# Input norm of a hybrid decoder layer: the reciprocal roots moved from VectorE's weighting into TensorE's transposing products

## The chip, the cores and the metric

The kernel runs on one core of one Trainium2 chip. The metric is device time in microseconds (us) of one execution. TensorE (PE in the rows) has a separate row for its weight loads (PEld); VectorE is DVE, ScalarE is ACT, GpSimd is POOL, and SyncE (SP) issues nearly all DMAs.

## The reference, cut to what matters

The reference is one decoder layer: 16 meta tokens and 512 real tokens of width 1024 are normalized, projected by one wide matrix, sent through sliding-window attention and a gated linear attention in parallel, merged, added to the stream, and then sent through a mixture of experts. The change concerns only the first step:

```python
def rms_norm(x, w):
    xf = x.astype(jnp.float32)
    y = xf * lax.rsqrt(jnp.mean(xf * xf, axis=-1, keepdims=True) + NORM_EPS)
    return (y * w.astype(jnp.float32)).astype(x.dtype)
...
    xn = rms_norm(h, norm1_w)
    proj = xn @ w_in
```

Each token (row) has one reciprocal root, and each of the 1024 columns has one weight. For the projection the kernel needs the normalized x transposed, with the 1024 columns on partitions.

## The kernel before, in words

The 512 real tokens are four blocks (b = 0 to 3) of 128 tokens, one token to a partition, held in `h`. The normalized stream is kept transposed and in two parts: `xhi`, x rounded to the fp32r format that TensorE multiplies in one pass, and `xlo`, the rest. Every projection is three products, hi by hi, hi by lo and lo by hi (lines 617 to 619).

All engines walk one list of steps, `SCHEDULE`, each engine in that order, and they meet only at semaphores. The list begins `xin`, `prep 0`, `xT`, `prep 1`, `xm 0`, then the first units of the projection. So an engine that waits in a step holds up all of its later steps.

- `xin` before the change. TensorE spreads the norm weights over 128 partitions (line 690), and ScalarE copies them to `norm1_b` (line 1271). For each block, ScalarE squares `h` and sums the squares (line 1275), VectorE turns the sum into mean plus epsilon (line 1575), GpSimd raises that to the power of -1/2 (line 1985, recorded at the helper's line 1952), and VectorE forms `xr = h * rstd * norm1_b` in one instruction (line 1578). VectorE does the means of blocks 0 and 1 ahead of `xr` of block 0, and after that the mean of block b + 1 ahead of `xr` of block b.
- `prep 0`: ScalarE and VectorE split the small gate weights into hi and lo (`gdp`, lines 1251 and 1567). `prep 1` splits the first wide chunk of weights, in two halves each.
- `xT`: for each block, TensorE transposes `xr` in eight 128x128 pieces, four to a PSUM bank (line 699); ScalarE copies each bank to `xhi` (line 1281), and VectorE writes the difference to `xlo` and so empties the bank (line 1585). Eight banks hold the eight halves.
- `xm`: the same for the meta tokens. ScalarE squares them after `prep 1`, GpSimd makes their root and then builds the rotary tables, VectorE scales them (line 1594), and TensorE transposes them after the first units (line 706).
- The first units (function `first_units`, lines 645 to 660) wait until all of `xhi` is there, and for a bank that line 1585 empties last.

DMAs: SP issues four loads of `h`, two weight chunks, the meta tokens and 16 small constants. Later weight chunks are issued when VectorE has done with the chunk whose buffer they take.

Of the kernel before, what the change touches and what calls it, by code (L numbers as in the profile page):

```python
# [21 lines left out]
ALU = mybir.AluOpType  # L22
ACT = mybir.ActivationFunctionType
# [3 lines left out]
D = 1024  # L27
T = 512
P = 128
NB = T // P  # L30
# [10 lines left out]
EPS = 1e-6  # L41
# [133 lines left out]
EARLY_DMAS = 2  # L175
# [89 lines left out]
def layer_kernel(nc, x, meta_tokens, norm1_w, w_in, q_norm_w, k_norm_w, attn_sinks, gla_gate_up, gla_gate_bias,  # L265
                 gla_norm_w, w_attn_branch, w_gla_branch, w_out, norm2_w, router_rows, norm2_rows,
                 expert_w_gate, expert_w_up, expert_w_down, table, triangle, rows_hbm, out):
    with ExitStack() as ctx:
# [3 lines left out]
        def sem(name):  # L272
            return ctx.enter_context(nc.semaphore(name))


        h = sb("h", [P, NB, D])
# [13 lines left out]
        stat = sb("stat", [P, 16])  # L290
        rstd = sb("rstd", [P, 16])
# [5 lines left out]
        ident = C("ident")  # L297
# [5 lines left out]
        def at(name, offset, shape, dt=F32):  # L303
            size = int(np.prod(shape[1:])) * 4
            assert offset + size <= arena_size, (name, offset, size, arena_size)
            return nc.alloc_sbuf_tensor_at(name, shape, dt, offset=arena_start + offset)

        K1 = 1024
# [5 lines left out]
        G = 82 * K1  # L314
# [30 lines left out]
        xr = at("xr", Y, [P, NB, D])  # L345
# [36 lines left out]
        norm1_b = at("norm1_b", G + 24 * K1, [P, D])  # L382
        norm1_1 = at("norm1_1", G + 28 * K1, [1, D])
        gdT = at("gdT", G + 64 * K1 + 256 + 4 * K1 + 512, [RANK + 1, XC])
        g_l = g_q1
        xj = at("xj", G + 32 * K1, [NM, D])
        reset = at("reset", Y + 16 * K1, [P, T])


# [47 lines left out]
        s_x = [sem(f"x{b}_loaded") for b in range(NB)]  # L437
        s_meta = sem("meta_loaded")
        s_early = sem("table_loaded")
# [14 lines left out]
        s_sumsq = sem("x_squares_summed")  # L454
        s_mean = sem("x_means")
        s_rstd = sem("x_rstd")
        s_xr = sem("x_scaled")
        s_xhi = sem("xT_hi")
        s_xlo = sem("meta_xT_lo")
        s_l = sem("log_terms")  # L460
# [152 lines left out]
        def _(pe):  # L613
# [15 lines left out]
            link = chain(pe, s_pe)  # L629
# [55 lines left out]
            for step in SCHEDULE:  # L685
                kind = step[0]
                if kind == "xin":
                    for half in range(2):
                        ps = banks.take(pe, "unit", ("norm1", half))
                        nc.tensor.matmul(ps[:, :], ones[0:1, :].bitcast(F32), norm1_1[:, half * 512:(half + 1) * 512],  # L690
                                         start=True, stop=True).then_inc(banks.done(("norm1", half)), 1)
                elif kind == "xT":
                    for b in range(NB):
                        pe.wait_ge(s_xr, b + 1)
                        for half in range(2):
                            ps = banks.take(pe, "x", ("xT", b, half))
                            for k in range(4):
                                src = xr[:, b, :].rearrange("p (c k) -> p k c", k=KT)[:, 4 * half + k, :]
                                last = nc.tensor.transpose(ps[:, k * P:(k + 1) * P], src, ident)
                            last.then_inc(banks.done(("xT", b, half)), 1)  # L700
                elif kind == "xm" and step[1] == 1:
                    pe.wait_ge(s_xr, NB + 1)
                    ps = banks.take(pe, "T", "xmT")
                    for k in range(KT):
                        src = xm[:, :].rearrange("p (c k) -> p k c", k=KT)[:, k, :]
                        last = nc.tensor.transpose(ps[:, k * NM:(k + 1) * NM], src, ident[0:NM, 0:NM])
                    last.then_inc(banks.done("xmT"), 1)
                elif kind == "unit":
# [17 lines left out]
                    if name == "gd":  # L726
                        ps = banks.take(pe, "unit", step)
                        last = mm3(ps[0:RANK, 0:NM], cols(gd_hi, 0, RANK), cols(gd_lo, 0, RANK),
                                   cols(xm_hi, 0, NM), cols(xm_lo, 0, NM), KT)
                    elif meta:  # L730
                        ps = banks.take(pe, "unit", step)
                        last = mm_packed(ps[0:PACK, 0:n], xpm, cols(wh, 0, n), cols(wl, 0, n))
                    elif name in ("qg", "ga", "gg", "kg"):
                        ps = banks.take(pe, "unit", step)
                        a, b = u * P, (u + 1) * P
                        last = mm3(ps[:, :], cols(wh, a, b), cols(wl, a, b), cols(xhi, xa, xb), cols(xlo, xa, xb), KT)
                    elif name in ("vg", "kva", "qa", "rg"):
                        ps = banks.take(pe, "unit", step)
                        a, b = NM + u * P, NM + (u + 1) * P
                        last = mm3(ps[:, 0:n], cols(xhi, a, b), cols(xlo, a, b), cols(wh, 0, n), cols(wl, 0, n), KT)  # L740
                    elif name in ("wa", "wg"):
                        if u == 0 and c0 == 0:
                            for b in range(NB):
                                pe.wait_ge(*banks.emptied(("ogT" if name == "wg" else "oT", b)))
                        ih, il = (oghi, oglo) if name == "wg" else (ohi, olo)
                        ps = banks.take(pe, "unit", step)
                        last = mm3(ps[:, :], cols(wh, u * P, (u + 1) * P), cols(wl, u * P, (u + 1) * P),
                                   cols(ih, 0, T), cols(il, 0, T), 4)
                    else:
                        ps = banks.take(pe, "unit", step)  # L750
                        last = mm3(ps[:, 0:n], tokens(mhi, u), tokens(mlo, u),
                                   cols(wh, 0, n), cols(wl, 0, n), KT)
                    last.then_inc(banks.done(step), 1)
                elif kind == "gates":
# [3 lines left out]
                    ps = banks.take(pe, "unit", ("z", j))  # L758
                    nc.tensor.matmul(ps[:, :], gate_up[:, j * P:(j + 1) * P], gdT[:, NM:XC],
                                     start=True, stop=True).then_inc(banks.done(("z", j)), 1)  # L760
# [3 lines left out]
                    ps = banks.take(pe, "T", "zm")  # L764
                    for j in range(2):
                        last = nc.tensor.matmul(ps[:, j * NM:(j + 1) * NM], gate_up[:, j * P:(j + 1) * P],
                                                gdT[:, 0:NM], start=True, stop=True)
                    last.then_inc(banks.done("zm"), 1)
                elif kind == "kdm":
                    pe.wait_ge(s_exp, 5)  # L770
                    ps = banks.take(pe, "T", "kdm")
                    for j in range(2):
                        last = nc.tensor.transpose(ps[0:NM, j * P:(j + 1) * P], lm[:, j, :], ident)
# [434 lines left out]
        def _(act):  # L1208
# [29 lines left out]
            for step in SCHEDULE:  # L1238
# [27 lines left out]
                elif kind == "xin":  # L1266
# [5 lines left out]
                                             ACT.Copy).then_inc(banks.read(("norm1", half)), 1)  # L1272
                    for b in range(NB):
                        act.wait_ge(s_x[b], 16)
                        nc.scalar.activation(xr[:, b, :], h[:, b, :], ACT.Square,
                                             accum_out=stat[:, b:b + 1]).then_inc(s_sumsq, 1)
                elif kind == "xT":
                    for b in range(NB):
# [217 lines left out]
        def _(dve):  # L1496
# [59 lines left out]
            for step in SCHEDULE:  # L1556
# [11 lines left out]
                elif kind == "xin":  # L1568
                    for half in range(2):
                        dve.wait_ge(*banks.emptied(("norm1", half)))  # L1570
                    for b in range(NB):
                        for ahead in (0, 1) if b == 0 else (b + 1,):
                            if ahead < NB:
                                dve.wait_ge(s_sumsq, ahead + 1)
                                nc.vector.tensor_scalar(stat[:, ahead:ahead + 1], stat[:, ahead:ahead + 1], 1.0 / D, EPS,
                                                        ALU.mult, ALU.add).then_inc(s_mean, 1)
                        dve.wait_ge(s_rstd, b + 1)
                        nc.vector.scalar_tensor_tensor(xr[:, b, :], h[:, b, :], rstd[:, b:b + 1], norm1_b[:, :],
                                                       ALU.mult, ALU.mult).then_inc(s_xr, 1)
                elif kind == "xT":  # L1580
                    for b in range(NB):
                        for half in range(2):
# [364 lines left out]
        def _(pool):  # L1947
# [3 lines left out]
            def tt(o, a, b, op=ALU.mult):  # L1951
                return nc.gpsimd.tensor_tensor(o, a, b, op)  # L1952
# [26 lines left out]
            for step in SCHEDULE:  # L1979
                kind = step[0]  # L1980
                if kind == "xin":
                    pool.wait_ge(s_set, 2)
                    for b in range(NB):
                        pool.wait_ge(s_mean, b + 1)
                        tt(rstd[:, b:b + 1], stat[:, b:b + 1], minus_half[:, b:b + 1], ALU.pow).then_inc(s_rstd, 1)
                elif kind == "xm" and step[1] == 0:
                    pool.wait_ge(s_mean, NB + 1)
                    tt(rstd[0:NM, NB:NB + 1], stat[0:NM, NB:NB + 1], minus_half[0:NM, 0:1], ALU.pow).then_inc(s_rstd, 1)
                    pool.wait_ge(s_early, EARLY_DMAS * 16)
                    pool.wait_ge(s_const, (CONST_DMAS - EARLY_DMAS) * 16)  # L1990
# [128 lines left out]
```

## Time and profile before

| | us |
|---|---|
| median of 3 runs (665.67 to 666.65) | 665.88 |
| the profiled execution's own time | 665.99 |
| its span, first to last instruction | 664.2 |
| TensorE busy | 644.5 |
| VectorE busy | 390.1 |
| ScalarE busy | 214.6 |
| GpSimd busy | 107.8 |

The span is 1.8 us shorter than the execution's own time; what lies around it is outside the profile. The page gives for each engine its busy time, its share of the span and its number of instructions. A row of the timeline reads: start, duration, engine, line, operation, output<-inputs, shape, count, and in brackets the idle time before it and what ended it. Rows of neighbouring instructions of the same kind are merged, with their count behind an x.

### The profile page before, as it was taken

What the parts mean: (1) busy time and instruction counts of PE and PEld (TensorE: products, weight loads), DVE (VectorE), ACT (ScalarE), POOL (GpSimd) and SP (SyncE); (2) the same over time, 40 slices, a digit from 0 to 9 for tenths busy, and PEclk for the clock granted to TensorE, in tenths of its full rate; (3) what the DMA queues carried; (4) which work ended last, traced back from release to release, by engine and by line L of the source; (5) the groups of instructions that cost most, each with busy time, mean ns of one, the idle gap of its engine ahead of it and who ended that gap; (6) DMA issues with size and microseconds to landing.
All of it is one profiled execution on the core that took longest, in us unless ns stands there. A gap on an engine that the chain in (4) does not pass through costs nothing.

```text
span 664.2 us, 10048 instructions
## 1 busy us (share of the span) xinstructions
PE 644.5 (97%) x3887; PEld 459.1 (69%) x3887; DVE 390.1 (59%) x721; ACT 214.6 (32%) x436; POOL 107.8 (16%) x168
## 2 busy tenths in 40 slices
PE   5799999999999999999989999999999999999998
PEld 3579999998787878778789995454444445453535
DVE  4648335688997979776765567444353535261605
ACT  6346222224444343432435475202020111110112
POOL 3300006899400000000000010201010101010010
PEclk9899999999999999999999999999999999999999
DMA  7432222302232211111554076999999999999943
GB/s 246 151 126 65 64 65 77 114 1 64 65 104 81 70 65 63 64 64 64 172 195 174 33 282 241 419 399 423 400 422 395 420 398 420 406 415 406 415 183 126
DMA packets 49793, 138.77 MB, mean 209 GB/s; under 512 B 6202, under 2 KB 28235, under 8 KB 41556
## 3 DMA queue, kind: packets, MB, share of 16 engines
q1 hardware_dynamic: 47298, 134.44, 53.1%
q0 software_dynamic: 2304, 3.64, 1.5%
q8 instruction: 31, 0.51, 0.3%
q14 instruction: 14, 0.11, 0.0%
q10 hardware_dynamic: 146, 0.07, 0.0%
HBM read 138.69 MB, written 4.19 MB: 215 GB/s over the span
## 4 chain that ended last, share of the span: by engine, by line
PE 87%; DVE 6%; ACT 3%; issue 2%; DMA 1%; POOL 0%; ACTq 0%; DVEq 0%
PE bank L1008 16%; PE bank L617 13%; PE bank L618 12%; PE bank L619 12%; PE bank L1022 8%; PE bank L1132 8%; PE bank L859 1%; DVE y_lo L1928 1%; PE bank L1033 1%; PE bank L961 1%; PE bank L892 1%; PE bank L927 1%; ACT whi L1251 1%; DVE sig_a L1637 1%; DVE sig_a L1633 1%
## 5 line engine op out<-in xcount | busy, mean ns | idle before, releaser
L1008 PE MATMUL bank<-w_pair,xgT 128*64 128x512 f32 x512 | 113.8, 596 | 0.0
L1008 PEld LDWEIGHTS bank<-w_pair,xgT 128*64 128x64 f32 x512 | 35.2, 137 | 66.4 <-issue 65.4
L1567 DVE TENSOR_TENSOR wlo<-wraw,whi 128x2048 fp32r<-128x2048 f32 (+1 forms) x25 | 56.4, 2258 | 19.9 <-ACT whi L1251 19.9
L617 PE MATMUL bank<-whi,xhi 128*128 128x256 f32 x224 | 64.4, 287 | 0.0
L619 PE MATMUL bank<-whi,xlo 128*128 128x256 f32 x224 | 62.9, 281 | 0.0
L618 PE MATMUL bank<-wlo,xhi 128*128 128x256 f32 x224 | 62.9, 281 | 0.0
L617 PE MATMUL bank<-xhi,whi 128*128 128x512 f32 x152 | 62.3, 410 | 0.0
L618 PE MATMUL bank<-xlo,whi 128*128 128x512 f32 x152 | 60.1, 395 | 0.0
L619 PE MATMUL bank<-xhi,wlo 128*128 128x512 f32 x152 | 59.7, 393 | 0.0
L1022 PE MATMUL bank<-w_pair,hT 128*64 128x512 f32 x256 | 58.1, 595 | 0.0
L1905 DVE SCALAR_TENSOR_TENSOR hg<-bank,pair_w,hs 128x256 f32<-128x256 f32 x16 | 7.7, 484 | 80.9 <-ACT hs L1472 80.9
L1251 ACT ACTIVATE whi<-wraw 128x2048 fp32r<-128x2048 f32 (+1 forms) x25 | 46.7, 1872 | 24.9 <-PE bank L626 11.1
L1472 ACT ACTIVATE hs<-bank 128x256 f32<-128x256 f32 x16 | 6.1, 383 | 135.6 <-PE bank L1008 135.6
L1941 DVE TENSOR_TENSOR h<-h,bank 128x512 f32<-128x512 f32 x64 | 41.4, 684 | 7.6 <-PE bank L1132 6.1
L1132 PE MATMUL bank<-y_hi,onehotT 128*128 128x512 f32 x112 | 44.2, 395 | 1.5 <-DVE y_lo L1928 1.5
L1132 PE MATMUL bank<-y_lo,onehotT 128*128 128x512 f32 x112 | 43.7, 390 | 0.0
L1928 DVE TENSOR_TENSOR y_lo<-bank,y_hi 128x512 fp32r<-128x512 f32 x32 | 20.6, 686 | 39.1 <-ACT y_hi L1485 39.1
L617 PEld LDWEIGHTS bank<-whi,xhi 128*128 128x128 f32 x224 | 42.1, 188 | 1.8 <-issue 1.4
L1952 POOL TENSOR_TENSOR pause<-pause 128x1 f32<-128x1 f32 x34 | 5.9, 195 | 223.2 <-PE bank L1002 184.2
L619 PEld LDWEIGHTS bank<-whi,xlo 128*128 128x128 f32 x224 | 42.2, 188 | 0.0
L618 PEld LDWEIGHTS bank<-wlo,xhi 128*128 128x128 f32 x224 | 42.1, 188 | 0.0
L1022 PEld LDWEIGHTS bank<-w_pair,hT 128*64 128x64 f32 x256 | 17.7, 137 | 33.3 <-issue 33.3
(333 smaller groups left out, 1304.7 us busy)
## 6 DMA issues: line engine op xcount, KB each, us to landing
w_pair<-in_expert_w_gate SPq DMA_DIRECT2D x32, 1024.0 KB
w_pair<-in_expert_w_up SPq DMA_DIRECT2D x32, 1024.0 KB
w_pair<-in_expert_w_down SPq DMA_DIRECT2D x32, 1024.0 KB, 17.5
wraw<-in_w_in SPq DMA_DIRECT2D x17, 1024.0 KB, 5.5
wraw<-in_w_out SPq DMA_DIRECT2D x4, 1024.0 KB, 5.1
h<-in_x SPq DMA_DIRECT2D x4, 512.0 KB, 5.1
wraw<-in_w_gla_branch SPq DMA_DIRECT2D x2, 1024.0 KB, 5.4
wraw<-in_w_attn_branch SPq DMA_DIRECT2D x2, 1024.0 KB, 5.1
```

Source lines behind the costliest of these rows:

```text
L617: nc.tensor.matmul(ps, lhi(k), rhi(k), start=(k == 0), stop=False)
L618: nc.tensor.matmul(ps, lhi(k), rlo(k), start=False, stop=False)
L619: last = nc.tensor.matmul(ps, llo(k), rhi(k), start=False, stop=(k == kt - 1))
L859: nc.tensor.matmul(ps[:, 0:width], q, k, start=True, stop=True).then_inc(banks.done(("S", b, i, j)), 1)
L1008: last = nc.tensor.matmul(tiles[GU_BANK[s]][j * SLOT:(j + 1) * SLOT, :].rearrange("p (f n) -> p f n", f=2), xgT[:, k, s * P + j * SLOT:s * ...
L1022: last = nc.tensor.matmul(tiles[DOWN_BANKS[s][half]][j * SLOT:(j + 1) * SLOT, :], hT[s][:, f, j * SLOT:(j + 1) * SLOT], we[s][j][2][:, f, ...
L1132: last = nc.tensor.matmul(tiles[SCATTER_BANKS[u % 4]][:, :], onehotT[i % 3][s][:, b, :], part[s][:, cols_], start=(s == 0 and part is y_hi ...
L1251: nc.scalar.activation(wh, raw, ACT.Copy).then_inc(s_hi, 1)
L1567: nc.vector.tensor_tensor(wl, raw, wh.bitcast(F32), ALU.subtract).then_inc(s_lo, 1)
L1905: nc.vector.scalar_tensor_tensor(hg[s][:, :], tiles[GU_BANK[s]][:, FF:2 * FF], pair_w[:, 2 * i + s:2 * i + s + 1], hs[s][:, :], ALU.mult, ...
L1928: last = nc.vector.tensor_tensor(y_lo[s][:, cols_], tiles[DOWN_BANKS[s][half]][:, :], y_hi[s][:, cols_].bitcast(F32), ALU.subtract)
L1941: nc.vector.tensor_tensor(h[:, b, cols_], h[:, b, cols_], tiles[bank][:, :], ALU.add).then_inc(s_add[u % 4], 1)
```

## The change: what it does and the diff

VectorE no longer waits for the roots: as soon as a block of x and the spread weights are there, it forms `xr = h * norm1_b`. ScalarE squares with a scale of 1/32, so that the sum is already the mean. GpSimd adds epsilon (a new tiny instruction), takes the power, and writes for each block a 128x128 matrix `diag` with the block's reciprocal roots on its diagonal (identity times root, spread over 128 columns). TensorE multiplies each piece of `xr` with `diag` where it had used its transpose operation with the identity. The result is the transposed piece with every token scaled. The squares go to a buffer of their own, since `xr` is now written at the same time.

```diff
+        x_sq = at("x_sq", G, [P, NB, D])
+        diag = at("diag", G + 16 * K1, [P, NB, P])
+        eps = at("eps", G + 18 * K1, [P, 1])
...
                     for b in range(NB):
                         pe.wait_ge(s_xr, b + 1)
+                        pe.wait_ge(s_diag, b + 1)
...
-                                last = nc.tensor.transpose(ps[:, k * P:(k + 1) * P], src, ident)
+                                last = nc.tensor.matmul(ps[:, k * P:(k + 1) * P], src, diag[:, b, :], start=True, stop=True)
...
-                        nc.scalar.activation(xr[:, b, :], h[:, b, :], ACT.Square,
+                        nc.scalar.activation(x_sq[:, b, :], h[:, b, :], ACT.Square, scale=D ** -0.5,
                                              accum_out=stat[:, b:b + 1]).then_inc(s_sumsq, 1)
...
                     for b in range(NB):
-                        for ahead in (0, 1) if b == 0 else (b + 1,):
-                            if ahead < NB:
-                                dve.wait_ge(s_sumsq, ahead + 1)
-                                nc.vector.tensor_scalar(stat[:, ahead:ahead + 1], stat[:, ahead:ahead + 1], 1.0 / D, EPS,
-                                                        ALU.mult, ALU.add).then_inc(s_mean, 1)
-                        dve.wait_ge(s_rstd, b + 1)
-                        nc.vector.scalar_tensor_tensor(xr[:, b, :], h[:, b, :], rstd[:, b:b + 1], norm1_b[:, :],
-                                                       ALU.mult, ALU.mult).then_inc(s_xr, 1)
+                        dve.wait_ge(s_x[b], 16)
+                        nc.vector.tensor_tensor(xr[:, b, :], h[:, b, :], norm1_b[:, :], ALU.mult).then_inc(s_xr, 1)
...
                 if kind == "xin":
                     pool.wait_ge(s_set, 2)
+                    pool.wait_ge(s_early, EARLY_DMAS * 16)
+                    link(nc.gpsimd.memset(eps[:, :], EPS))
                     for b in range(NB):
-                        pool.wait_ge(s_mean, b + 1)
+                        pool.wait_ge(s_sumsq, b + 1)
+                        link(tt(stat[:, b:b + 1], stat[:, b:b + 1], eps[:, :], ALU.add))
                         tt(rstd[:, b:b + 1], stat[:, b:b + 1], minus_half[:, b:b + 1], ALU.pow).then_inc(s_rstd, 1)
+                        pool.wait_ge(s_rstd, b + 1)
+                        tt(diag[:, b, :], ident, rstd[:, b:b + 1].to_broadcast([P, P])).then_inc(s_diag, 1)
                 elif kind == "xm" and step[1] == 0:
-                    pool.wait_ge(s_mean, NB + 1)
+                    pool.wait_ge(s_mean, 1)
```

`link` makes the engine wait for the instruction that it has just issued; the two waits of GpSimd inside a block (for the sum, for the root) therefore put its three instructions strictly one behind the other.

## Rows read from the trace of the kernel before

**Rows 1.** The page: busy time by engine, then shares of the chain that ended last.
```profile
PE 644.5 (97%) x3887; PEld 459.1 (69%) x3887; DVE 390.1 (59%) x721; ACT 214.6 (32%) x436; POOL 107.8 (16%) x168
PE 87%; DVE 6%; ACT 3%; issue 2%; DMA 1%; POOL 0%; ACTq 0%; DVEq 0%
```
**Rows 2.** The chain of waits from 9 us on: start, duration, what.
```profile
9.47 1.54 POOL rstd L1952
...
15.51 4.80 DVE xlo L1585 x8
...
20.44 3.32 PE bank L645 x8
...
31.45 0.98 PE bank L706 x8
```
**Rows 3.** Timeline of ScalarE and VectorE, 6 to 21 us.
```profile
6.54 0.60 ACT L1271 ACTIVATE norm_b<-bank 128x512 f32<-128x512 f32 x1 [1.11 <-PE bank L690]
7.98 0.19 ACT L1275 ACTIVATION_READ_ACCUMULATOR xr<-h 128x1 f32 x1
10.50 1.06 ACT L1275 ACTIVATE xr<-h 128x1024 f32<-128x1024 f32 x1 [0.18 <-DMA h<-in_x]
16.10 1.08 ACT L1281 ACTIVATE xhi<-bank 128x512 fp32r<-128x512 f32 x2 [0.26 <-PE bank L699]
...
8.32 0.15 DVE L1575 TENSOR_SCALAR stat<-stat 128x1 f32<-128x1 f32 x1 [6.97 <-ACT xr L1275]
9.31 1.28 DVE L1578 SCALAR_TENSOR_TENSOR xr<-h,rstd,norm_b 128x1024 f32<-128x1024 f32 x1
20.21 1.22 DVE L1563 TENSOR_TENSOR wlo<-wraw,whi 128x1024 fp32r<-128x1024 f32 x1
```
**Rows 4.** Timeline of GpSimd: a root alone, a root and a square product later.
```profile
8.63 0.57 POOL L1952 TENSOR_TENSOR rstd<-stat,minus_half 128x1 f32<-128x1 f32 x1 [6.57 <-DVE stat L1575]
27.09 0.40 POOL L1952 TENSOR_TENSOR tri_r<-k_tok 128x128 fp32r<-128x128 f32 x1
L1952 POOL TENSOR_TENSOR pause<-pause 128x1 f32<-128x1 f32 x34 | 5.9, 195 | 223.2 <-PE bank L1002 184.2 <-DVE row_no L1553 28.1 <-issue 9.8
```
**Rows 5.** Timelines where GpSimd and VectorE meet: 117 to 131 us, then 23 us.
```profile
117.77 1.66 POOL L1952 TENSOR_TENSOR rstd<-stat,minus_half 128x8 f32<-128x8 f32 x1 [7.29 <-DVE stat L1509]
125.75 3.52 POOL L1952 TENSOR_TENSOR rstd<-stat,minus_half 128x8 f32<-128x8 f32 x1 [0.96 <-DVE stat L1509]
...
125.49 2.29 DVE L1567 TENSOR_TENSOR wlo<-wraw,whi 128x2048 fp32r<-128x2048 f32 x1
127.69 0.29 DVE L1625 TENSOR_SCALAR rgs<-rgs 128x256 f32<-128x256 f32 x1
...
23.26 3.30 DVE L1594 TENSOR_SCALAR xm<-xm,rstd 16x1024 f32<-16x1024 f32 x1 [0.65 <-POOL rstd L1952]
23.20 2.81 POOL L1952 TENSOR_TENSOR tab<-cst,qk_w 128x256 f32<-128x256 f32 x4
```
**Rows 6.** Timeline of TensorE's weight loads and products, narrow stretches.
```profile
2.73 3.78 PE L690 MATMUL bank<-norm,ones 1*128 1x512 f32 x4 [2.73 <-DMA norm<-in_norm_w]
...
10.64 1.97 PE L699 MATMUL bank<-cst,xr 128*128 128x128 f32 x8 [4.14 <-DVE xr L1578]
10.92 1.30 PEld L699 LDWEIGHTS bank<-cst,xr 128*128 128x128 f32 x6
13.93 0.99 PEld L699 LDWEIGHTS bank<-cst,xr 128*128 128x128 f32 x8
15.36 1.16 PE L699 MATMUL bank<-cst,xr 128*128 128x128 f32 x8 [0.24 <-DVE xr L1578]
134.51 1.05 PE L818 MATMUL bank<-vg,att 128*128 128x128 f32 x8
```
**Rows 7.** Busy by engine, granted clock, DMA of a stretch; then TensorE's timeline.
```profile
20.80:24.20 3.40, 3.40 (x10) 1.86 (x9) 2.75 (x4) 0.00 (x0) 1.51 (x3) 0.50 0.84 280
...
25.72 1.55 PE L654 MATMUL bank<-xlo,gdp 128*48 128x512 f32 x6
```

More of the change, by code:

```diff
@@ L456, in layer_kernel @@
         s_rstd = sem("x_rstd")
-        s_xr = sem("x_scaled")
+        s_xr = sem("x_weighted")
+        s_diag = sem("x_rstd_diagonal")
         s_xhi = sem("xT_hi")
```

## The prediction, made before the changed kernel was run

> **What bounds the kernel now.** I read three views: the page, the chain of waits over the first 45 us, then the timelines of single engines between 6 and 33 us. The page says that TensorE is busy 97% of the span and carries 87% of the chain [rows 1]. So a change in the input norm can pay only through the stretch in which TensorE still waits. The chain shows it: up to 20.44 us the path runs over GpSimd's roots, VectorE's `xr`, and eight `xlo` differences in a row (15.51 + 4.80 = 20.3), and from 20.44 on over TensorE's products without a gap [rows 2]. What counts is when the gate products of line 645 start, and at which clock. Everything behind moves along: of the later suppliers the nearest, the scaled meta tokens, is there at 23.26 + 3.30 = 26.56 [rows 5] for a use at 31.45 [rows 2], and weight chunks are loaded and split relative to earlier steps.
>
> Inside that stretch VectorE is the late one. Its first `xr` starts at 9.31 [rows 3] though x and the weights have been there since 7.14 (6.54 + 0.60) [rows 3]. The last `xr` releases the last block's transposes at 15.36 [rows 6], and only then, at 15.51, do the eight `xlo` begin [rows 2], which stand behind `xr` in VectorE's order. Those transposes end at 15.36 + 1.16 = 16.52 [rows 6]: TensorE then idles 3.9 us, and its clock is at 0.50, which is 1.2 of its 2.4 GHz, from 20.8 to 24.2 us [rows 7].
>
> **Part 1: VectorE's `xr` moves ahead.** Four two-input products of 128x1024; the nearest row is line 1563, 1.22 us [rows 3]. They start at about 7.3, each about 0.08 before the last one's end (as line 1625 at 127.69 follows 125.49 + 2.29 = 127.78 [rows 5]), and block 3, landed at 10.50 [rows 3], is needed only at 10.7. Unhindered they run 7.29 to 8.51, 8.43 to 9.65, 9.57 to 10.79, 10.71 to 11.93, so the last is done 3.4 us earlier. Four means of 0.15 us [rows 3] go. The `xlo` then follow ScalarE's copies one by one and are no longer a queue of 4.8 us.
>
> **Part 2: GpSimd's chain per block.** One new 128x1 addition (0.20, from the 34 tiny additions [rows 4]), the root (0.57), and the diagonal (0.40, the row of a 128x128 product; its broadcast input is taken at the same rate) [rows 4], with two handoffs of some 0.08: 1.3 us per block if free. It isn't free. A root that takes 0.57 alone takes 1.54 when it begins at 9.47 under the `xr` that began at 9.31 [rows 2 to 4]: it ends at 11.01, 0.42 after that `xr` ends at 10.59. So a two-input VectorE instruction holds GpSimd off until its end, and GpSimd then needs its own time less about 0.14. After the change VectorE runs four of them back to back, exactly over block 0's three GpSimd instructions. What happens between two of them no row shows for two such instructions. Nearest is the root at 125.75: it ends at 129.27, which is 127.78 + 1.49, its free 1.66 less the usual 0.15, although line 1625 had started at 127.69; and that one took 0.29, so it was hardly held up [rows 5]. GpSimd was served at the boundary. I take that: one GpSimd instruction per boundary. The addition, released at 8.32 (7.98 + 0.19, and the handoff that VectorE's mean shows [rows 3]), runs after 8.51; the root, asked for during the second `xr`, after 9.65, to 10.07; the diagonal after 10.79, to 11.05. The fourth `xr` is pushed by at most 0.26, to 12.2. TensorE's first product starts at 11.15. Blocks 1 to 3 follow about 12.2 + 1.15, then every 1.3 us: 13.4, 14.7, 16.0.
>
> The Trainium skill (SBUF — State Buffer, Who interferes with whom) has the pair of ports held for the whole instruction, also by GpSimd against VectorE. By the skill the tiny additions and roots would hold up `xr` in full as well, and the first product would start at about 11.75, 0.6 later; the 0.29 us of line 1625 speaks against it for tiny operands.
>
> **Part 3: TensorE's products.** A transpose is one instruction per piece: 32 for 32 pieces. A plain f32 product is two: line 818 has four products in a block and 8 instructions, in 1.05 us [rows 6]. Their spacing is (1.05 - 0.275)/7 = 0.111 us, that of a transpose at full clock (0.99 - 0.19)/7 = 0.114 [rows 6]. So 64 instructions instead of 32: 7.1 us at full clock. At the low clock a transpose takes (1.30 - 0.23)/5 = 0.214 [rows 6]; the page's clock column says 1.00 there, but the spacing is the low one. It rose at about 13.9 us, 3.3 us after the first transpose at 10.64 [rows 6]. With C us of low clock the 64 take 7.1 + 0.48 C (1 - 0.111/0.214 = 0.48). With C = 3.3, as measured here: 8.7 us. GpSimd's 1.3 us a block is faster than TensorE's 1.8 to 3.4, so TensorE, not GpSimd, sets this stage once started. It ends at 11.15 + 8.7 + 0.17 (the last one's latency) = 20.0, against 16.52.
>
> The Trainium skill (TensorE: Matmul & The Clock Gate, Terms) calls the transpose mode four times as fast for f32. By the skill the 32 products would take 14.2 us instead of 7.1. The trace differs: twice the instructions at one spacing.
>
> **Part 4: from the last product to the gate products.** Before, ScalarE's last copy ended at 16.10 + 1.08 = 17.18, 0.66 after TensorE's end [rows 3, 6]. One difference (4.80/8 = 0.60, with its tail 0.68) [rows 2] and two handoffs of 0.1 follow: about 1.55 us. The gate products start at 20.0 + 1.55 = 21.55, that is +1.1 us. TensorE now idles 1.55 us and not 3.9, so I expect the clock to stay high. The 3.40 us at 0.50 hold eight starts of 0.415 to 0.43 us each (3.32/8 [rows 2], the first of them still at full clock). At full clock products of 512 columns are (1.55 - 0.39)/5 = 0.232 apart [rows 7], so the same work takes 1.85: -1.55 us.
>
> **Sum.** +1.1 - 1.55 = -0.45 us on the profiled execution's 665.99, so 665.5, a fraction under the median of the runs, 665.88. A measurement of this kernel tells about 0.2% (1.3 us) from no change, so this is no change. What VectorE gains, TensorE's doubled instructions and GpSimd's chain eat; what remains is the clock.
>
> Bounds. C from 0 (clock already risen) to 6.6 (twice the measured rise; the four products at 2.73 to 6.51 [rows 6] show that 3.8 us of work need not leave it high) gives -1.6 to +1.6 around it, so 663.9 to 667.1 for this case alone.
>
> **The rivals.**
>
> *A, GpSimd starved, slower.* VectorE's four `xr` go through without letting GpSimd in. For it: the roles reversed, a small VectorE instruction at 23.26 took 3.30 us beside four GpSimd products back to back, 2.81 us [rows 5], so it lost three boundaries. Against it: 125.75. Then GpSimd's addition starts at 11.93, the first diagonal is ready at 13.25, products run 13.35 to 22.2, the gate starts at 23.75: +3.3 - 1.55 = +1.75, 667.7. It decides from two lost boundaries on.
>
> *B, GpSimd hardly held up.* If one-element reads slip in beside `xr`, the diagonal is there at 9.65 and the products run to 18.5, the gate starts at 20.1: -0.35 - 1.55 = -1.9, 664.1. Against it: the root at 9.47 with its 1.54 us [rows 2]. For it: only that VectorE's instruction is now another kind.
>
> *C, the clock.* It rises late or falls again before the gate products: +1.1 with the 1.55 not won, 667.1. For it: two low stretches in the first 25 us. Against it: the idle time before the gates is less than half.
>
> *D, the product costs four instructions.* 64 more at 0.111: +7.1, 672.6. Line 818 speaks against it.
>
> **How the numbers follow.** Chances: forecast 0.50, A 0.22, B 0.17, C 0.09, D 0.02. Faster by over 0.2%: 0.15 of B and 0.05 of the forecast (an early rise of the clock) = 0.20. Slower by over 0.2%: 0.17 of A (+0.26%, just beyond), 0.06 of C, 0.02 of D, 0.03 of the forecast with a late clock = 0.28. Within: 0.52. The range takes in B, A with a slightly late clock, and leaves D: 664.0 to 668.3.
>
> **What would show each step.** Part 1: the four `xr` start before 11 us and the last ends by 12.3. Part 2: the first root of GpSimd lasts about 1.0 to 1.5 us, and the first diagonal ends near 11.05; near 13.3 it is A, near 9.7 B. Part 3: line 699 has 64 instructions, 0.111 or 0.214 apart, without waits for GpSimd after the first block, ending near 20. Part 4: the gate products start 1.5 us behind that, 0.23 apart from the first. Wrong altogether: if VectorE's `xlo` is still what the gate waits for with a queue behind it, or if the time changes behind 40 us.

## The result: slower by 1.1%, and the profile after

| | before | after |
|---|---|---|
| median of four runs, us | 666.26 (665.67 to 667.04) | 673.92 (672.48 to 674.12) |
| the profiled execution's own time, us | 665.99 | 674.12 |
| its span, us | 664.2 | 672.3 |

The ratio is 1.0106, with a 95% interval of 1.0090 to 1.0121. That is 7.7 us more, where the prediction had 0.45 us less and a range that ended at 668.3. First the head of the page, the lines that answer to [rows 1]: busy times and instructions of each engine, then the shares of the chain.

```profile
span 672.3 us, 10121 instructions
PE 654.3 (97%) x3919; PEld 469.4 (70%) x3919; DVE 390.4 (58%) x717; ACT 214.9 (32%) x436; POOL 110.4 (16%) x177
PE 89%; DVE 5%; ACT 3%; issue 2%; DMA 1%; POOL 0%; ACTq 0%; DVEq 0%; POOLq 0%
```

TensorE has 32 instructions more, as forecast (3919 against 3887), but 9.8 us more busy time, which is 0.31 us for each of them. (A "product" below, with its count behind an x, is one such instruction; a plain f32 product of one piece is two of them.) The chain of waits of the changed kernel over its first 50 us (start, duration, what) tells where; it answers to [rows 2]:

```profile
7.15 1.04 ACT x_sq L1280 x2
8.33 0.20 POOL stat L1951
8.60 1.45 POOL rstd L1951
10.11 0.89 POOL diag L1951
...
11.14 15.51 PE bank L704 x64
26.67 0.61 ACT xhi L1286
27.30 0.70 DVE xlo L1584
...
28.14 3.03 PE bank L649 x8
31.17 2.40 PE bank L653 x8
...
39.12 0.98 PE bank L711 x8
40.10 0.43 PE bank L621
```

The reader is to see that VectorE's queue of eight `xlo` is gone from the path and that one stretch of TensorE has taken its place: 64 products in 15.51 us, where 8.9 were forecast. The gate products (now line 649) start at 28.14 instead of 20.44, 7.70 later. The last gate preparation, line 711, starts at 39.12 instead of 31.45 [rows 2], 7.67 later, and everything behind it is moved by that much; up to 329 us the shift stays at 7.68 us. There a single wait adds 0.5: TensorE stands idle for 1.28 us instead of 0.76 behind a chunk of output weights that landed 5.6 us after its issue instead of 5.1, and from there on the shift is 8.2. So nearly all of the loss is made before 28 us.

The timeline of GpSimd and VectorE (start, duration, engine, line, operation, names, shape, count, and in brackets the idle time before and its end) shows that all ahead of the products went as forecast:

```profile
8.60 1.44 POOL L1951 TENSOR_TENSOR rstd<-stat,minus_half 128x1 f32<-128x1 f32 x1
10.11 0.88 POOL L1951 TENSOR_TENSOR diag<-cst,rstd 128x128 f32<-128x128 f32 x1
10.96 1.16 POOL L1951 TENSOR_TENSOR stat<-stat,eps 128x1 f32<-128x1 f32 x1
12.84 0.40 POOL L1951 TENSOR_TENSOR diag<-cst,rstd 128x128 f32<-128x128 f32 x1
15.35 0.40 POOL L1951 TENSOR_TENSOR diag<-cst,rstd 128x128 f32<-128x128 f32 x1
...
7.24 4.83 DVE L1578 TENSOR_TENSOR xr<-h,norm_b 128x1024 f32<-128x1024 f32 x4 [5.89 <-ACT norm_b L1276]
```

Then line 704 by itself: PEld is the loading of the weights (the stationary operand, here a piece of `xr`), PE the product; durations in ns as lowest/median/highest, then the first and last start. The first two lines are the whole stage, the third its products up to 15 us, the fourth those behind:

```profile
L704 PEld LDWEIGHTS bank<-diag,xr x64: 312/336/338, 11.1 to 26.1; 128*128 128x128 f32 x64
L704 PE MATMUL bank<-diag,xr x64: 345/402/577, 11.1 to 26.2; 128*128 128x128 f32 x64
L704 PE MATMUL bank<-diag,xr x16: 442/444/577, 11.1 to 14.9; 128*128 128x128 f32 x16
L704 PE MATMUL bank<-diag,xr x46: 401/402/403, 15.3 to 26.0; 128*128 128x128 f32 x46
```

Two rows of the kernel before belong beside them; the prediction used neither. The first is its transposes of the same `xr`, the second the row that my price came from:

```profile
L699 PEld LDWEIGHTS bank<-cst,xr x32: 186/198/230, 10.6 to 16.1; 128*128 128x128 f32 x32
L818 PEld LDWEIGHTS bank<-vg,att x32: 188/192/192, 134.4 to 159.5; 128*128 128x128 f32 x32
```

A weight load of the new products takes 0.336 us, one of line 818 0.192, and one of the transposes 0.198 at the median, of the same operand. (That the piece is the weights in a transpose too shows in the row of the meta tokens' transposes, line 706, whose form is `16*128 16x16`: weights of 16x128 against an identity of 16x16.) From start to start the new products are 0.238 us apart, (26.2 - 11.1)/63 = 0.24 from the row's ends, against 0.111. They keep that distance at both clocks, though a single one is shorter once the clock has risen (0.402 for 0.444). The granted clock has little to do with this stage; the weight load has: 0.336 us at either clock.

Last, stretches of the changed kernel: the length, then busy time and number of instructions of PE, PEld, DVE, ACT, POOL, then the granted clock, the DMA share and GB/s.

```profile
15.20:20.20 5.00, 5.00 (x23) 5.00 (x23) 1.90 (x3) 1.79 (x3) 0.48 (x2) 1.00 0.39 95
26.70:28.10 1.40, 0.00 (x0) 0.00 (x0) 0.69 (x1) 1.40 (x2) 0.00 (x0) 1.00 0.00 0
28.90:32.20 3.30, 3.30 (x9) 2.05 (x8) 2.65 (x4) 1.29 (x3) 1.46 (x3) 0.50 0.08 10
```

TensorE idles only 1.5 us between products and gates, against 3.9 before, and still its clock is at 0.50 (1.2 of 2.4 GHz) behind it, as in [rows 7]. This is so in three of the four runs (mean granted clock of the span 0.997); the fourth, at 1.000, had no fall and is the one at 672.48, about 1.45 us below the others.

### The profile page after: what moved, and what is told of

It is laid out like the page before. It is cut to its first block, busy times and chain, and to the rows that moved or that the text cites. A ratio compares the mean times of both kernels' runs of the same rounds, so it can differ in the third digit from the quotient of the medians.

```text
span 672.3 us, 10121 instructions
## 1 busy us (share of the span) xinstructions
PE 654.3 (97%) x3919; PEld 469.4 (70%) x3919; DVE 390.4 (58%) x717; ACT 214.9 (32%) x436; POOL 110.4 (16%) x177
## 4 chain that ended last, share of the span: by engine, by line
PE 89%; DVE 5%; ACT 3%; issue 2%; DMA 1%; POOL 0%; ACTq 0%; DVEq 0%; POOLq 0%
PE bank L1013 16%; PE bank L621 12%; PE bank L622 12%; PE bank L623 12%; PE bank L1027 8%; PE bank L1137 8%; PE bank L704 2%; PE bank L864 1%; DVE y_lo L1927 1%; PE bank L1038 1%; PE bank L966 1%; PE bank L897 1%; PE bank L932 1%; ACT whi L1256 1%; DVE sig_a L1636 1%
## 5 line engine op out<-in xcount | busy, mean ns | idle before, releaser
L1256 ACT ACTIVATE whi<-wraw 128x2048 fp32r<-128x2048 f32 (+1 forms) x25 | 46.7, 1871 | 25.0 <-PE bank L630 11.1
```

The source lines that it names most:

```text
L1256: nc.scalar.activation(wh, raw, ACT.Copy).then_inc(s_hi, 1)
```

## The experiments

Theory: a plain f32 product loads `xr` slowly because the 128 columns that it takes as weights lie eight f32 elements (32 bytes) apart, `"p (c k) -> p k c"` with k = 8; TensorE's transpose of the same operand does not pay this, nor does line 818, whose columns lie side by side. Rivals: the products wait for GpSimd or share something with it; or a plain product of this kind costs this much in this place whatever the layout.

### e1: the columns side by side, VectorE reading at a step of eight

```diff
-  src = xr[:, b, :].rearrange("p (c k) -> p k c", k=KT)[:, 4*half+k, :]
+  src = xr[:, b, :].rearrange("p (h c l) -> p h l c", h=8, l=1)[:, 4*half+k, 0, :]
-  tensor_tensor(xr[:, b, :], h[:, b, :], norm1_b, mult)
+  # xr written piece by piece, h and norm1_b read as "p (c h l) -> p h c l"
```

> The changed kernel, but VectorE writes xr piece by piece, so that the 128 columns of a piece lie side by side (step of 1 element instead of 8) for TensorE's weight load. Theory S (the load of f32 weights at a step of 8 elements sets the 0.238 us of a diagonal product): weight loads fall from 0.335 to about 0.19 us, the products to 0.111 us apart at the full clock, the stage ends near 20.0 instead of 26.6 us, and the time is about 666 to 667.5 us. Rival K (the kind of the product sets it: a plain f32 product that opens its own region, against a diagonal just written): still 0.238 apart, about 673.5 us. Either way VectorE's xr may take longer than 1.22 us each for its step of 8 elements in reading; over 1.6 us each, the first product starts later.

Measured: 668.17 against 666.08 of the kernel before, ratio 1.0033 (1.0022 to 1.0044). The weight loads (all, then those up to 16.5 us, at the low clock), the chain's entry of the products, and VectorE's and GpSimd's rows:

```profile
L704 PEld LDWEIGHTS bank<-diag,xr x64: 192/192/338, 13.5 to 22.2; 128*128 128x128 f32 x64
L704 PEld LDWEIGHTS bank<-diag,xr x15: 288/333/338, 13.5 to 16.4; 128*128 128x128 f32 x15
13.53 9.03 PE bank L704 x64
7.24 8.06 DVE L1578 TENSOR_TENSOR xr<-h,norm_b 128x1024 f32<-128x1024 f32 x4 [5.88 <-ACT norm_b L1276]
9.40 2.25 POOL L1953 TENSOR_TENSOR rstd<-stat,minus_half 128x1 f32<-128x1 f32 x1
```

The products fell from 15.51 to 9.03 us, 0.111 apart at full clock and 0.214 at the low one, with the same diagonals and the same number of instructions. At the low clock a load takes 0.333 us here too, so there the layout costs next to nothing (0.240 apart against 0.214); what the eight-element step loses is the gain of the full clock, 0.192 us a load. VectorE pays for it: 2.0 us per block instead of 1.2, and GpSimd, which is served at VectorE's boundaries, is later with it. The first product starts 2.4 us later, and with that the time lies 0.7 us above the range that I had expected.

### e2: the columns four elements apart

```diff
+  # as e1 with h=2, l=4: the columns of a piece lie 16 bytes apart
```

> The changed kernel with xr laid out so that the columns of a piece are 4 elements apart (16 bytes) instead of 8. Theory S, with the cost growing with the step: the spacing lies between 0.111 and 0.238 us, about 0.12 to 0.15 if it is the 16-byte line that counts (the Trainium skill, SBUF — State Buffer, has steps up to 4 f32 elements free; by the skill 0.111), time 666 to 669 us. Rival K: 0.238 apart, about 673.5 us.

Measured: 672.78 against 666.08, ratio 1.0090 (1.0073 to 1.0107).

```profile
L704 PEld LDWEIGHTS bank<-diag,xr x64: 309/330/330, 11.1 to 25.8; 128*128 128x128 f32 x64
11.11 15.19 PE bank L704 x64
```

At 16 bytes the products are 0.233 apart, nearly as at 32 and not between the two, as I had expected. VectorE's side is as cheap as in the changed kernel (first product at 11.11).

### e3: the kernel before, its transposes made plain products

```diff
-  nc.tensor.transpose(tiles[...], src, ident)
+  nc.tensor.matmul(tiles[...], src, ident, start=True, stop=True)
```

> The kernel before with one word changed: its transposes are plain f32 products with the same identity, from the same xr at a step of 8 elements. Nothing else of the change. Theory S: 64 instructions 0.238 us apart, from 10.64 us on without a wait for VectorE: 10.64 + 15.3 + 0.2 = 26.1, gate products from 27.7 us on, so about +7 us: 672.5 to 674 us. Then the whole loss is the product's. Rival: the diagonal (the other operand, or GpSimd's writes to it) is what slows the products; then they are 0.111 to 0.214 apart here and the time is within 1.5 us of 666.

Measured: 672.23 against 666.08, ratio 1.0083 (1.0066 to 1.0100): one word in the kernel before brings 6.2 of the 7.7 us.

```profile
L699 PEld LDWEIGHTS bank<-cst,xr x64: 312/335/340, 10.7 to 25.6; 128*128 128x128 f32 x64
10.65 15.53 PE bank L699 x64
```

There is no diagonal here, and GpSimd's chain is the old one. Its stretch of 15.53 us is the changed kernel's 15.51. Both rivals with GpSimd (waiting for it, or sharing something with it) fall.

### e4: the changed kernel, its products made transposes

```diff
-  nc.tensor.matmul(tiles[...], src, diag[:, b, :], start=True, stop=True)
+  nc.tensor.transpose(tiles[...], src, ident)
```

> The changed kernel with the transposes by the identity kept: the scaling by the reciprocal roots is left out of the real tokens, the rest of the change (VectorE early, GpSimd's diagonals, TensorE's wait for them) stays. It shows what the change's VectorE and GpSimd parts are worth without the doubled products. Transposes 0.111 to 0.214 us apart, one block per 1.3 us behind the diagonals at 11.05, 13.25, 14.5, 15.75, ending near 16.8 to 17.5; gate products from 18.4 to 19.1 us, 1.3 to 2 us earlier than before: 664 to 665 us, and up to 1.5 us more or less by whether TensorE's clock falls before the gate products.

This kernel leaves out the scaling by the roots. Measured: 664.33 against 666.08, ratio 0.9971 (0.9958 to 0.9983). The chain now waits for GpSimd once more and for three `xlo`, and the gates start at 19.77:

```profile
L704 PEld LDWEIGHTS bank<-cst,xr x32: 185/226/226, 11.2 to 17.6; 128*128 128x128 f32 x32
13.52 3.57 PE bank L704 x16
17.74 1.90 DVE xlo L1584 x3
19.77 2.03 PE bank L649 x8
```

So the reordering of VectorE and GpSimd alone is worth 1.75 us. In the profiled execution, which is 2.4 us shorter than that of the kernel before, 0.67 is the earlier gates (19.77 against 20.44) and 1.55 the clock, which did not fall behind them (30.20 - 19.77 = 10.43 us to the first unit, against 11.98); by their mean clock it did fall in two of the six. The whole loss hangs on what TensorE does. e2 and e4 together leave e1's reading: the distance of the columns, for plain products alone.

### e5: the columns side by side, VectorE writing at a step

```diff
+  src = xr[:, b, (4*half+k)*P:(4*half+k+1)*P]
+  tensor_tensor(xr[:, b, :].rearrange("p (k c) -> p c k", k=KT), h[:, b, :] ("p (c k) -> p c k"), norm1_b (same), mult)
```

> As e1_step1 (the 128 columns of a piece side by side in xr), but VectorE walks h and the weights in their order and scatters what it writes, where in e1 it read both at a step of 8 elements and took 2.0 us a block. Theory: it is VectorE's reading at a step that cost 0.8 us a block; writing at a step is free, so xr takes 1.22 us as in the changed kernel, the first product starts at 11.14 and with products 0.111 us apart (0.214 before the clock rises) the stage ends at 19.8 to 21.5 us. The prediction's sum with the layout mended: gate products at 21.4 to 23 us, time 665 to 667 us. Rival: writing at a step costs VectorE as much as reading: first product at 13.5, time as e1, 668.2 us.

Measured: 668.26 against 665.97, ratio 1.0029 (1.0020 to 1.0038).

```profile
7.19 7.47 DVE L1578 TENSOR_TENSOR xr<-h,norm_b 128x1024 f32<-128x1024 f32 x4 [5.84 <-ACT norm_b L1276]
13.01 10.28 PE bank L704 x64
```

My theory that only VectorE's reading at a step costs was wrong, and the rival right: side by side in reading but 512 bytes apart in writing it takes 1.87 us a block. The first product is at 13.01, and the whole is worth what e1 is.

### e6 and e11: the columns two elements apart

```diff
+  # as e1 with h=4, l=2: the columns of a piece lie 8 bytes apart
```

> The changed kernel with the columns of a piece 2 elements apart. With steps of 8 and 4 at 0.238 and 0.233 us and a step of 1 at 0.111: if a 16-byte line is loaded once and serves all of its columns, 2 elements (two columns a line) are as good as 1: 0.111 us, about 666.5 us. If every step over 1 breaks the load: 0.233 us, about 673 us. A value between, near 0.17, means a cost per line.

> e6_step2 (the changed kernel with nothing but the columns of a piece 2 elements apart) timed in rounds. It is the prediction's sum with its mis-sized term mended: 64 products at 0.118 us, first product at 11.1, gate products near 21.5 to 22.5. Theory that the weight load was the only wrong step of size: 665.5 to 666.8 us, no difference from before that can be told. Rival (something else of the change costs as well): over 667 us.

Measured: e6, one run, 666.29. e11, eleven runs, 666.52 against 666.16, ratio 1.0004 (0.9995 to 1.0013). Rows of e11: its weight loads, and its chain.

```profile
L704 PEld LDWEIGHTS bank<-diag,xr x64: 196/196/336, 11.2 to 20.0; 128*128 128x128 f32 x64
11.21 9.14 PE bank L704 x64
20.38 0.61 ACT xhi L1286
21.01 0.70 DVE xlo L1586
21.85 2.01 PE bank L649 x8
```

At 8 bytes the products are 0.118 apart, and VectorE stays at 4.83 us for its four. This is the changed kernel with one size mended. Its products start at 11.21, its gates at 21.85, at full clock (2.01 us for eight), where the prediction had 11.15 and 21.55; no change was forecast, and none is measured.

### e7: the norm weights read from PSUM

```diff
+  # e5's layout; ScalarE's copies of the spread weights left out
+  tensor_tensor(xr half, h half, banks.get(("norm1", half)), mult)   # 8 in place of 4
```

> As e5, and VectorE reads the spread norm weights from the two PSUM banks in which TensorE left them, in halves of 512 columns (8 instructions), so that it has one SBUF input only; ScalarE's two copies to norm1_b go. Theory (GpSimd is held off by VectorE's second SBUF input): GpSimd's root takes 0.56 and the diagonal 0.40 us beside xr, the first diagonal is ready near 9.7 instead of 11.0 and the first product starts 1.4 us earlier than in e5; time about 1 to 1.4 us below e5, 664 to 665.5 us. Rival (any VectorE instruction holds GpSimd off): root 1.4 us as before, no gain over e5.

Measured: 663.77 against 665.97, ratio 0.9959 (0.9945 to 0.9972). VectorE's eight products, GpSimd's first root and diagonal, then the chain:

```profile
5.86 7.33 DVE L1576 TENSOR_TENSOR xr<-h,bank 128x512 f32<-128x512 f32 x8 [4.51 <-DMA h<-in_x]
7.42 0.57 POOL L1957 TENSOR_TENSOR rstd<-stat,minus_half 128x1 f32<-128x1 f32 x1
8.07 0.40 POOL L1957 TENSOR_TENSOR diag<-cst,rstd 128x128 f32<-128x128 f32 x1
...
8.62 9.43 PE bank L704 x64
19.54 2.02 PE bank L649 x8
```

With only one of its inputs in SBUF and the other in PSUM, the memory that TensorE writes to, VectorE no longer holds GpSimd off: the root takes the 0.57 that it takes alone [rows 4], in the midst of VectorE's products. All twelve of GpSimd's instructions in this stage keep their free durations (0.18 to 0.57), so it isn't that shorter VectorE instructions have more boundaries. The gain over e5, 4.5 us, is several times the 1 to 1.4 that I expected; the squares too start 1.3 us earlier, since ScalarE has nothing to copy ahead of them.

### e8: the price of the low clock

```diff
+  # kernel before, in TensorE's idle 3.9 us ahead of the gates:
+  pe.wait_ge(*banks.emptied(("xT", 0, 0)))
+  for _ in range(4):
+      nc.tensor.matmul(tiles[3][:, :], ident, h[:, 0, 0:512], start=True, stop=True)   # never read
```

> The kernel before, with four products of 512 columns that nobody reads, issued by TensorE behind the last block's transposes (the identity by 512 columns of h, into a bank already emptied), in the 3.9 us in which it idles. Theory (the idle time lets the clock fall before the gate products, which then cost 1.55 us more): no stretch at 0.50 from 20.8 to 24.2, time 1.3 to 1.6 us below before, 664.5 us. Rival (the clock doesn't follow this idle time, or the extra products delay the gate products): within 0.4 us of before, or slower.

Measured: 664.28 against 665.97, ratio 0.9967 (0.9955 to 0.9979). The stretch answers to that of [rows 7], with 17 products where it had 10:

```profile
20.80:24.20 3.40, 3.40 (x17) 2.27 (x16) 2.75 (x4) 0.00 (x0) 1.48 (x3) 1.00 0.91 291
20.49 2.00 PE bank L645 x8
```

Nothing else moved: the gates start at 20.49 (20.44 before), the first unit of line 617 at 30.90 and not 32.42. The price that the prediction put on the low stretch, 1.55 us, is what was measured, 1.5 in the trace and 1.7 in the time. (Seven of the sixteen executions of the kernel before have a mean clock of 0.995 and a median of 666.64; against the nine at 0.997, the profiled one's kind, with a median of 665.74, the time too says 1.5.)

### e9 and e10: towards a faster kernel

```diff
+  # e9: e6's layout, e7's weights from PSUM, and four unread products of a block of ones ahead of the pieces
+  # e10: kernel before, no diagonals; scalar_tensor_tensor with norm1 from PSUM in halves, and e8's products
```

> The version that the earlier runs point to: the changed kernel with columns 2 elements apart (e6), the weights read from PSUM by VectorE (e7), and four products that nobody reads between the spreading of the norm weights and the first diagonal product. From e7 (first product 8.6, clock risen 4.1 us later, end 18.0, gate products 19.54): theory that the idle time ahead keeps the clock low: it rises 1 to 2 us earlier, the stage ends 0.5 to 1 us earlier, and the time is 0.5 to 1 us below e7's 663.8. Rival: the rise doesn't follow this activity; then as e7, within 0.3 us, plus 0.006 us for each of the products at a step of 2 (0.118 against 0.111), 664.

> The kernel before with the two additions that helped but without the diagonal products: VectorE reads the norm weights from PSUM in its scaling, and TensorE is kept busy between its transposes and the gate products (e8). GpSimd's roots are then no longer held off (0.57 us each instead of 1.54), VectorE's first xr starts near 7.7, the last one by block 3's arrival at 13.0 to 13.9, the eight xlo end near 18.9: gate products 1 to 1.4 us earlier than in e8, time 662.9 to 663.5 us. If it lies at or below e9, the diagonal products are worth nothing here even with the layout mended.

Measured: e9 664.73 against 666.16, ratio 0.9973 (0.9961 to 0.9984); e10 663.36, ratio 0.9957 (0.9943 to 0.9971). Chain of e9, then of e10:

```profile
8.51 8.80 PE bank L706 x64
18.80 2.01 PE bank L649 x8
```

```profile
16.54 3.44 PE bank L703 x8
19.97 1.84 PE bank L645 x8
```

e9's gates start 0.74 us ahead of e7's, and TensorE is still 0.59 us ahead at the end. But its time is 1.0 us longer than e7's, where 0.5 to 1 us less was expected. In the profiled execution it is lost at the output stores: of the 128 part landings that eight stores report, 125 were there by 660.75 us, and three came at 661.27, 661.89 and 662.51; e7's were all there by 661.35. Why is open, and only this execution has a trace. The nine spans fall in two groups, 660.7 to 661.1 (three runs) and 662.7 to 663.8 (six), and two of the first three lose as much outside the span (3.1 and 3.3 us there instead of 1.8). e10 has no product with a diagonal and is as fast as e7 within the intervals. So the diagonals, even well laid out, are not shown to bring anything that the reordering, PSUM and a busy TensorE don't bring without them.

## Why the prediction was wrong, point by point

**Part 1 held.** Four `xr` from 7.24 to 12.07 us; forecast 7.29 to between 11.93 and 12.2.

**Part 2 held.** From the root on GpSimd is served at VectorE's boundaries, once each: the addition at 8.33, the root to 10.04, the diagonal to 10.99, the first product at 11.14; forecast 8.51, 10.07, 11.05, 11.15. The later diagonals end at 13.24 and 15.75; forecast 13.4 and 16.0. That the addition ran at 8.33, while the first `xr` was on until about 8.5, is the one small miss; it changed nothing, since the root behind it still waited for the boundary of the second `xr`. Rivals A (first products at 13.35) and B (at 9.65) are out. In e1 and e5 the same happened with longer VectorE instructions (roots of 2.25 and 2.10 us), and in e7 the cause was taken away.

**Part 3 failed, in one term: "64 instructions at 0.111 us".** Their number was right and their spacing wrong, 0.238. The stage took 15.51 us for 8.87 (8.7 and 0.17), so the gates start 6.6 us later than forecast. The spacing came from line 818, and what I did not compare is the operand's layout, which stands in the code: line 818's weights lie side by side, those of `xr` 32 bytes apart. The transposes of [rows 6] seemed to clear the layout, since they take the same operand at 0.114. But they are another mode, and e3 shows in one word of code that this is what shielded them. The clock's term, 0.48 C, was wrong with it: with such weights the products keep to 0.24 us at either clock, where those with side-by-side columns go from 0.214 to 0.111 when it rises (e1). Mending the layout alone (e11) brings 9.14 us for the stage and 666.52 for the whole.

The Trainium skill's factor of four for the transpose mode (TensorE: Matmul & The Clock Gate, Terms), from which the prediction worked out 14.2 us for the 32 products, comes near the 15.2 us measured (64 by 0.238), but not as a rule: a piece costs 2 x 0.238 = 0.476 us against 0.111 by transpose, a factor of 4.3, at steps of eight columns, and 2 x 0.111 = 0.222, a factor of 2, with the columns side by side (e1). The rule that bears on the layout is in the Trainium skill (SBUF — State Buffer, Door 1: The DMA port swizzle): SBUF is read in lines of 16 bytes, a line should be hit at least twice, and a stride of up to four f32 is called free. The first half agrees with every plain product here at full clock: two hits per line at a step of two (0.118), one at four (0.233) and at eight (0.238). It does not agree with the transposes, which have one hit per line and load in 0.19 to 0.23 us (e4). The last does not agree either, since four is as slow as eight. I had not weighed it for TensorE's weights.

**Rival D's size, not its mechanism.** 672.6 was its time, 0.02 its chance. The product is two instructions, not four; each is twice as long.

**Part 4 was right in its first term and failed in its second.** From the end of the products to the gates it took 28.14 - 26.65 = 1.49 us; forecast 1.55. But the clock fell all the same, in three of four runs, and from the gates to the first unit it is 40.10 - 28.14 = 11.96 us, as before (32.42 - 20.44 = 11.98), not 10.4. That is rival C, with the 1.55 not won. Its price was right (e8). Its condition was not the idle time alone: all kernels of this study but the one before, e4, e8 and e10 leave about 1.5 us there. Of those whose products are 0.233 to 0.238 apart at full clock (after, e2, e3) 7 of 12 runs had the fall, by their mean clock; of those at 0.111 to 0.118 (e1, e5, e6, e7, e9, e11) none of 45. With 1.8 us of idle time behind transposes (e4) it was 2 of 6, and with 3.9 (before) every run. The idle time was varied alone by e8: filled, the fall was gone in all six runs. The layouts of e1, e2 and e11 keep the idle time at 1.5 us, but where they quicken the products they also shorten the stage by 6 us. So the falls behind 1.5 us go with slowly loaded products; that these are the cause is not shown.

**The sum.** 665.54 + 6.6 (part 3) + 1.55 (part 4) = 673.7 for the profiled execution, against 674.12. The remaining 0.4 us are, within 0.1, the one longer wait at 329 us. The prediction had named a change behind 40 us as a sign of being wrong altogether; this one is small, and the same wait differs between the other profiles as well (from 1.1 us in e8 to 1.75 in e11, start to start), so nothing ties it to the change.

## What to carry to other kernels

Take the price of a TensorE instruction only from a row with the same mode, type and layout of the stationary operand, and look for its LDWEIGHTS row: here plain f32 weights want their columns at most two elements apart, while the transpose forgave the one step that was tried, eight. When a fused step is traded for cheaper ones elsewhere, check the layout that the old form tolerated, and choose one that suits both sides: a step of two cost neither VectorE nor TensorE anything (e11), a step of one cost VectorE 0.65 to 0.8 us a block (e1, e5). And where an engine waits for another at the pair of inputs in SBUF, moving one input to PSUM (e7) can be worth more than the change of algorithm.

## What the runs showed of the hardware that I had not expected

- Weight loads of plain f32 128x128 products: at full clock 0.192 us at a step of 4 bytes between columns, 0.196 at 8, 0.330 at 16, 0.336 at 32 (e1, e11, e2, after). At the low clock all four take 0.33 to 0.34, so the wide steps lose what the full clock gives. The transpose: 0.186 to 0.230 at 32.
- A two-input VectorE product of 128x1024 in f32: 1.21 us side by side or in pairs, 2.0 when both inputs are read 32 bytes apart (e1), 1.87 when the output is written 512 bytes apart (e5).
- TensorE's clock fell after 1.5 us of idle time behind slowly loaded products, and rose 3.0 to 6.3 us after the first piece in the profiles of this study, without an order by kernel: 3.0 in e11, 3.3 before, 3.4 in e1, 4.1 in e3 and after, 5.5 in e8, 6.1 in e2, 6.3 in e10. Only e9, with unread products ahead of its first piece, was earlier, 2.4. A stage at this place of the kernel has, as an estimate, about 1.6 us of uncertainty from that alone (0.48 x 3.3).
- Removing 0.6 us from TensorE's path doesn't always arrive at the end: in the profiled run of e9 three of the 128 part landings of the output stores were late, the last by 1.8 us.
